# Adaptive modulation computed beside the first layer's projection instead of in a stage of its own

## The reference

```python
for layer in range(DEPTH):                      # DEPTH = 2
    mod_l = (silu(c) @ w_ada[layer] + b_ada[layer])[:, None, :]
    mod_c = (silu(c_ctx) @ w_ada[layer] + b_ada[layer])[None, None, :]
    sh_ml, sc_ml, gt_ml, sh_fl, sc_fl, gt_fl = split(mod_l, 6, axis=-1)
    ...
    a_lat = rmsnorm(h_lat, g_mix[layer]) * (1 + sc_ml) + sh_ml
    a_ctx = rmsnorm(h_ctx, g_mix[layer]) * (1 + sc_mc) + sh_mc
    # layer 0
    cq, ckv, kr, qs, ks, vs = split_last(a @ w_in, [384, 256, 32, 512, 128, 128])
    q = rmsnorm(cq, g_q) @ w_uq                 # 8 heads of 64 + 32
    kv = rmsnorm(ckv, g_kv) @ w_ukv             # 8 heads of 64 + 64
    ...
```

## Time and profile before

| | us |
|---|---|
| median of 3 runs | 3107.32 |
| lowest and highest of them | 3104.43, 3111.47 |
| the profiled execution | 3107.07 |
| its span, first to last instruction | 3105.3 |
| the modulation stage ends, the next stage's first DMA is issued | 160.5, 165.7 |
| first product of `chunk(0, 0)` | 178.2 |
| first product of the attention of layer 0 | 374.0 |

### The profile page before, as it was taken

How to read it: one execution, slowest core, us unless ns; L and a number is a source line. 1 busy time by engine, 2 the same in 40 slices (tenths; PEclk the granted TensorE clock), 3 DMA queues, 4 the chain that set the end, 5 groups by cost and what they waited for, 6 DMA issues and landing times. The chain is left out here.

```text
span 3105.3 us, 37707 instructions
## 1 busy us (share of the span) xinstructions
PE 2736.1 (88%) x12450; PEld 1942.5 (63%) x12450; DVE 1725.1 (56%) x2132; ACT 1462.1 (47%) x2059; POOL 991.4 (32%) x697
## 2 busy tenths in 40 slices
PE   7979999987879999999994679997779999999990
PEld 2345677775457676666772668885547677667660
DVE  7923244543745555656563855555465566565546
ACT  5612233431146666666662344444126666666650
POOL 1000000012345555555551000001235555555542
PEclk9989999998989999999997789998889999999995
DMA  9930100023059999999995611102329999999966
GB/s 349 354 119 14 41 1 1 1 78 151 6 208 379 386 387 370 375 373 375 382 340 190 250 55 37 37 11 85 149 76 367 374 365 342 362 348 346 358 251 257
DMA packets 160999, 694.89 MB, mean 224 GB/s; under 512 B 34776, under 2 KB 46040, under 8 KB 100752
## 3 DMA queue, kind: packets, MB, share of 16 engines
q1 hardware_dynamic: 116240, 607.41, 52.0%
q0 software_dynamic: 43520, 84.21, 7.1%
q10 hardware_dynamic: 1152, 2.11, 0.2%
HBM read 678.82 MB, written 86.08 MB: 246 GB/s over the span
## 5 line engine op out<-in xcount | busy, mean ns | idle before, releaser
L1571 DVE TENSOR_TENSOR F_gu_lo<-gu_raw,F_gu_hi 128x2048 fp32r<-128x2048 f32 x292 | 662.2, 2291 | 589.3 <-ACT F_gu_hi L1516 580.3
L1516 ACT ACTIVATE F_gu_hi<-gu_raw 128x2048 fp32r<-128x2048 f32 x292 | 554.2, 1918 | 71.8 <-DMA gu_raw<-in_we_up_dram 47.7
L1465 PE MATMUL F_psY<-d_raw,F_hT 128*128 128x512 f32 x1168 | 525.6, 593 | 2.9 <-ACT F_hT L1534 2.9
L102 PE MATMUL F_psG<-F_gu_hi,F_xT_hi 128*128 128x512 f32 x1168 | 470.5, 403 | 6.9 <-DVE F_xT_lo L1563 6.9
L104 PE MATMUL F_psG<-F_gu_hi,F_xT_lo 128*128 128x512 f32 x1168 | 458.0, 392 | 0.0
L103 PE MATMUL F_psG<-F_gu_lo,F_xT_hi 128*128 128x512 f32 x1168 | 456.5, 391 | 0.0
L1391 POOL DMA_INDIRECT F_xb<-f_d,F_gi x146 | 339.4, 2325 | 130.5 <-POOL F_gi L1388 120.5
L1465 PEld LDWEIGHTS F_psY<-d_raw,F_hT 128*128 128x128 f32 x1168 | 211.2, 191 | 212.9 <-issue 209.5
L1530 ACT ACTIVATE F_yb<-F_psY,wgt 128x1024 f32<-128x1024 f32 x146 | 163.1, 1117 | 362.2 <-PE F_psY L1465 362.2
L1388 POOL COPY F_gi<-gat 128x1 int32 (+1 forms) x146 | 303.4, 2078 | 15.4 <-PE F_psX L1448 15.1
L102 PEld LDWEIGHTS F_psG<-F_gu_hi,F_xT_hi 128*128 128x128 f32 x1168 | 221.7, 190 | 49.2 <-DVE F_xT_lo L1563 8.3
(11 more groups left out here) (335 smaller groups left out, 4430.3 us busy)
## 6 DMA issues: line engine op xcount, KB each, us to landing
gu_raw<-in_we_gate_dram SPq DMA_DIRECT2D x146, 1024.0 KB, 9.0
gu_raw<-in_we_up_dram SPq DMA_DIRECT2D x146, 1024.0 KB
d_raw<-in_we_down_dram SPq DMA_DIRECT2D x146, 1024.0 KB, 6.9
wada<-in_w_ada_dram SPq DMA_DIRECT2D x24, 2048.0 KB, 11.2
I_ring<-y_d SPq DMA_DIRECT2D x24, 1024.0 KB, 7.0
H_y<-y_d SPq DMA_DIRECT2D x4, 4096.0 KB, 18.9
I_w_raw<-in_wc_in_dram SPq DMA_DIRECT2D x32, 384.0 KB, 3.3
f_d<-D_f SPq DMA_DIRECT2D x10, 512.0 KB, 2.6
```

Of the source, the lines that this page charges most:

```text
L102: nc.tensor.matmul(acc, xh, wh, start=(start and i == 0), stop=False)
L1465: ins = nc.tensor.matmul(psY[:, n], hT[:, j, k], d_raw[:, j, k, c], start=(k == 0), stop=(k == KF - 1))
L1516: nc.scalar.activation(gu_hi[:, j, v], gu_raw[:, j, v], ACT.Copy).then_inc(s_guh, 1)
L1571: V.tensor_tensor(gu_lo[:, j, v], gu_raw[:, j, v], gu_hi[:, j, v].bitcast(F32), ALU.subtract).then_inc(s_gul, 1)
```

## The change

`stage_modulation` and the barrier behind it are gone. `stage_front(t_, wq0)` takes the place of both stages.

- The two condition vectors stand in a zero-padded stationary operand `cs`, 128 x 32 for each of the 8 slices of the contraction, in plain fp32. There is no high and low half.
- The work is cut into 48 steps: six groups of 2048 output columns (`QUADS`), each over 8 slices of the contraction (`KD`). A step reads one 128 x 2048 piece of `w_ada` (1 MB). It is four matmuls with 512 columns each, whose results go to partitions 0 to 31, 32 to 63, 64 to 95 and 96 to 127 of one PSUM bank `psM`.
- The first group, which is shift and scale of layer 0, goes first; its 8 MB have a buffer of their own, `wq0`. The other 40 steps stand one behind each product of the projection from product number 8 on (`step(g)` at the end of `chunk`). They read from a ring of two 1 MB buffers, which are tiles 2 to 5 of `h`. So `x` and `ctx` are read tile by tile into `h[:, t % 2]`, and once more, whole, at the start of `stage_attend0`, ahead of the sink values in SP's list.
- Shift and scale are no longer broadcast over partitions. The projection turns the normalized tile first; shift and scale, turned once by four PE transposes into `mc`, are applied per partition while the turned tile is brought out of PSUM, four slices by ACT and four by DVE. POOL's addition goes.
- `up(t, 0)` and `up(t, 1)` are split in two products each (`Q0`, `Q1` of 384 columns, `K0`, `K1` of 512), and share a three-buffer `psC` with the chunks. `psU` goes. One stage now has 48 products, eight for each tile.
- Bias and store of a group go through SP. The gains are loaded by POOL.

```diff
-        stage_modulation()
-        end_stage()
...
-                stage_project0(t_)
+                stage_front(t_, wq0)
...
+            QN, QUADS, RING = 2048, 6, 2
+            STEPS = QUADS * KD
...
+                cs = sb(ctx, "B_cs", [P, KD, 32])
...
-                psC = ps(ctx, "B_psC", [P, 2, 512])
+                psC = ps(ctx, "B_psC", [P, 3, 512])
...
-                psU = ps(ctx, "B_psU", [P, 1024])
...
+                ring = [h[:, 2:4].rearrange("p t d -> p (t d)"), h[:, 4:6].rearrange("p t d -> p (t d)")]
...
+                        def rows(t):
+                            if t >= 2:
+                                sp.wait_ge(s_an, t - 1)
...
+                            sp.dma_start(h[:, t % 2], src).then_inc(s_hin[t % 2], 16)
...
+                        for i in range(KD, STEPS):
+                            q, k = divmod(i, KD)
+                            if i == 10:
+                                rows(4)
+                            if i == 17:
+                                rows(5)
+                            if k == 4 and q >= 1:
+                                if q >= 2:
+                                    store(q - 1)
+                                else:
+                                    sp.wait_ge(s_mrow, q)
+                                load_bias(q)
+                            r = (i - KD) % RING
+                            if i - KD >= RING:
+                                sp.wait_ge(s_stp, i - RING + 1)
+                            sp.dma_start(ring[r], w_ada(i)).then_inc(s_rg[r], 16)
...
-                            nc.gpsimd.tensor_tensor(an[:], an[:], aadd[:], ALU.add).then_inc(s_an, 1)
...
-                                ins = nc.scalar.activation(aT[:], src, ACT.Copy)
...
+                                for k in range(KD // 2):
+                                    ins = nc.scalar.activation(aT[:, k], src[:, k], ACT.Identity, scale=mc[:, v, KD + k:KD + k + 1], bias=mc[:, v, k:k + 1])
...
-                            nc.vector.scalar_tensor_tensor(an[:], h[:, t], st[:, 0, 2:3], amul[:], ALU.mult, ALU.mult).then_inc(s_an0, 1)
+                            V.tensor_scalar(an[:], h[:, t % 2], st[:, 0, 2:3], None, ALU.mult).then_inc(s_an, 1)
...
+                        def step(i):
+
+                            q, k = divmod(i, KD)
...
+                            for j in range(4):
+                                ins = nc.tensor.matmul(psM[32 * j:32 * j + 32], cs[:, k], w[:, j * 512:(j + 1) * 512], start=(k == 0), stop=(k == KD - 1))
+                            ins.then_inc(s_stp, 1)
...
+                            if g >= KD:
+                                step(g)
...
+                        for k in range(KD):
+                            step(k)
+                            if k == 5:
+                                turn("A", 0)
+                        pe.wait_ge(s_mrow, 1)
+                        for c in range(4):
+                            ins = nc.tensor.transpose(psM[:, c * P:(c + 1) * P], mrow[:, c * P:(c + 1) * P], ident)
+                        ins.then_inc(s_mt, 1)
...
+                        sp.dma_start(h[:, 0:NL], a["x"][0].rearrange("(t p) d -> p t d", p=P)).then_inc(s_h, 16)
+                        sp.dma_start(h[:, NL:NT], a["ctx"][0].rearrange("(t p) d -> p t d", p=P)).then_inc(s_h, 16)
                         sp.dma_start(sink[:], a["wa_sink"][0:1, :].to_broadcast([P, 8])).then_inc(s_sink, 16)
```

More of the change, by code:

```diff
@@ L146, in kview @@
             return w.rearrange("(p k) n -> p k n", p=P)
[L149 to L270, removed]
-                            if i == WB:
-                                dve.wait_ge(s_cst, 16)
-                                nc.vector.tensor_copy(ident_b[:], ident)
-                                nc.vector.tensor_copy(mask_b[:, 0], cst[:, C_MP:C_MP + P])
-                                nc.vector.tensor_copy(mask_b[:, 1], cst[:, C_MN:C_MN + P])
-                        out_of(2 * NCH - 1)
@@ new lines, in w_ada, with store @@
+                        def w_ada(i):
+                            q, k = divmod(i, KD)
+                            return a["w_ada"][q // 3].rearrange("(p k) n -> p k n", p=P)[:, k, q % 3 * QN:(q % 3 + 1) * QN]
+                        def store(q):
+                            sp.wait_ge(s_mrow, q + 1)
+                            for v in range(2):
+                                sp.dma_start(mod_d[q // 3, v, q % 3 * QN:(q % 3 + 1) * QN].rearrange("(g n) -> g n", n=512),
+                                             mrow[v:P:32]).then_inc(s_mout, 16)
@@ new lines, in load_bias @@
+                        def load_bias(q):
+                            for v in range(2):
+                                sp.dma_start(bias[v:P:32], a["b_ada"][q // 3, q % 3 * QN:(q % 3 + 1) * QN].rearrange("(g n) -> g n", n=512)).then_inc(s_b, 16)
+                        sp.dma_start(craw[:, 0, :], a["c"][0].rearrange("(p k) -> p k", p=P)).then_inc(s_c, 16)
+                        sp.dma_start(craw[:, 1, :], a["c_ctx"].rearrange("(p k) -> p k", p=P)).then_inc(s_c, 16)
+                        sp.dma_start(wq0[:, 0], w_ada(0)).then_inc(s_q0[0], 16)
@@ new lines, in _, with w_chunk @@
+                        sp.dma_start(cst[:], a["cst"]).then_inc(s_cst, 16)
+                        rows(0)
+                        for k in range(1, KD):
+                            sp.dma_start(wq0[:, k], w_ada(k)).then_inc(s_q0[k], 16)
+                            if k == 1:
+                                sp.wait_ge(s_zero, 3)
+                                load_bias(0)
+                        wv = a["wa_in"][0].rearrange("(k p) n -> p k n", p=P)
+                        def w_chunk(i):
+                            c0, n = chunks[i]
@@ L372, in _ @@
+                        store(QUADS - 1)
+                        sp.wait_ge(s_mout, 32 * (QUADS - 1))
                     @block.gpsimd
                     def _(pool):
-                        for t in range(NT):
-                            pool.wait_ge(s_an0, t + 1)
-                            nc.gpsimd.tensor_tensor(an[:], an[:], aadd[:], ALU.add).then_inc(s_an, 1)
+                        nc.gpsimd.memset(cs[:], 0.0).then_inc(s_zero, 1)
+                        nc.gpsimd.memset(bias[:], 0.0).then_inc(s_zero, 1)
@@ L414, in evac @@
                             ins.then_inc(s_tev, 1)
+                        act.wait_ge(s_zero, 3)
+                        act.wait_ge(s_c, 32)
+                        for v in range(2):
+                            ins = nc.scalar.activation(cs[:, :, v], craw[:, v, :], ACT.Silu)
+                        ins.then_inc(s_silu, 1)
+                        act.wait_ge(s_cst, 16)
                         norm(0)
@@ L543, in _ @@
                                 chunk(s, 3)
-                                up_q(s)
+                                chunk(s, "Q0")
+                                chunk(s, "Q1")
                     @block.tensor
```

270 lines of the change are left out of this document (173 added, 97 removed).

## The result

The changed kernel took 3027.02 us (median of 4 runs, 3023.88 to 3031.44) against 3109.39 us for the kernel before (4 runs). The ratio is 0.9736 with a 95% interval of 0.9721 to 0.9750: 82 us faster, where 27 were forecast. Repeated on another chip, the pair gave 3025.5 and 3107.8 us, 0.9732 (0.9717 to 0.9747).

The account below looks back on a forecast made before the run. DMA was taken to bound the modulation and PE the projection. Against 3107.07 us, -142.4 + 85.8 + 13.1 - 7.1 + 14 + 1 + 8.3 = -27.3 gave 3080 us, range 3025 to 3140.

Parts of the forecast that it names:

- the full overlap of the groups: Rival for the modulation steps on PE: all four column groups stream side by side, step 0.86 us, total 3033 us; chance 0.26.
- the stepwise one: Main case for the modulation steps: PE's program order lets column groups overlap only partly, 2.15 us a step, 3080 us; chance 0.46.
- the price of a step: Forty modulation steps added to PE's list in the projection, 2.15 us each, +85.8 us; ends +34 and +137.
- Going over: PE switching between full-width products and column groups, charged 0.33 us a step: +13.1 us, bounds 0 and +21.
- The front: Everything ahead of the first projection product: `chunk(0, 0)` starts at 35.8 us instead of 178.2, -142.4 us.
- The waits for `psU`: PE's waits in the projection for DVE to empty `psU`, 5.6 + 1.5 us, go: -7.1 us.
- The stall at piece 17: In SP's list `rows(5)` waits for `norm(3)` ahead of piece 17; PE stands 11 us, with low clock +14 us (8 to 17).
- piece 10: `rows(4)` ahead of this piece in SP's list has the same form; 10.3 of 11.2 us are covered, +1 us.
- The sink values: At the attention's start their small load waits behind 3.15 MB of `x` and `ctx` on SP: +8.3 us (0 to 9.1).
- The ring getting tight: Under full overlap, close projection products leave 5 us for a piece: +1 us a tile, +5 us.
- The band of 3064 to 3094 for the likeliest case: Span of total time for partly overlapping groups, 3080 us, with all small terms at their ends; chance 0.46.
- a warm PE: Small term at the projection's start, set at zero: the first chunk may find PE's clock up, up to -3 us.

Follow-up runs that it names:

- pair experiment: Changed kernel with its first eight steps run in pairs of two contraction slices, pairs 0 and 2 slice by slice, 1 and 3 group by group: 3031.2 us in one run.

## Why the prediction was wrong, point by point

The direction was right and the measured time lies in the range, 2 us above its lower end. But the forecast of 3080 us was the wrong case: the full overlap of the groups, at 0.26, held, and not the stepwise one at 0.46. The range was drawn to take in that rival, so that it holds says nothing for the mechanism.

- **The step that failed is the price of a step**: "I take the middle", 2.15 us, +85.8. It rested on two readings of the rows: a product is two records (true: 320 records for 160 products in the forty steps), and full-width records start in program order (true, but no evidence on groups: each of those products writes all 128 partitions, so in none of them was there another group that could have gone ahead). The pair experiment shows that groups don't wait for one another. A step streams for 0.86 us, +34.3. That is 51.5 of the 55 us between the gain forecast, 27.3, and the one measured, 82.4. The prediction set two statements of the Trainium skill's page "TensorE: Matmul & The Clock Gate" against each other. The speedup of 2.38 times for three column groups, in its section "Measured speedup vs the span model", points the right way: four groups here take 0.99 against 3.43 us, 3.5 times. The statement of the same page of the Trainium skill, in "The mechanism", that matmuls start in program order did not hold here for two products per group: the first record of the next group started 14 ns behind the first of its predecessor, ahead of three records that stand before it.
- **Going over**, +13.1 from two tails of 0.163: 0.28 us a step, +11.3. The size is right. It doesn't show in the step's own row alone: 0.13 us of it lies there and the rest in what stands behind. The tail is the difference to a modelled end, so that it comes so close may be luck.
- **The front**, -142.4: -144.4. The last piece was taken up at 28.5 us, a microsecond ahead of the estimate, with DMA at 342 and 392 GB/s instead of 306 and 379. The chain from there to the first product took 5.3 us instead of 6.3. (The 379 GB/s are not in the earlier trace rows; they are the kernel before's rate from 20 to 40 us.)
- **The waits for `psU`**, -7.1: gone.
- **The stall at piece 17**, +14, and piece 10, +1: 10.4 and 1.5 us of wait and about 2 of low clock. The run with the loads moved takes 14.7 us out of the projection and has neither wait. Right, by the mechanism named.
- **The sink values**, +8.3: the attention is 8.0 us longer than before, PE's wait 8.8. Right, in size and mechanism: with the order undone the attention takes 8.1 or 10.9 us less in the two traces.
- **The ring getting tight** under full overlap, +5: no such wait; a piece landed in 4.7 us (median of 40), and the two tightest places leave about 5. That rival's 3033 was 6 us too high, 5 of it by this term.
- The sum for the projection with measured terms: 195.8 + 34.3 + 11.3 + 12.0 + 2 - 7.1 = 248.3 us, which is what it took. The 2 us of low clock are mainly the step and the turns behind the wait, 1.93 and 1.94 us instead of 1.06 and 1.08. The going over was itself taken from the length of one tile, so the sum tests only that the other tiles are like it.
- The band of 3064 to 3094 for the likeliest case does not follow from its terms. With the going over and the sink values at nothing, the stall at 8 and a warm PE it reaches down to about 3050.

What makes the later stages differ by 8 us between the two profiled executions is open. The same stages spread by 12 us over the traces of kernels that don't differ in them.

## What to carry to other kernels

A stage held by DMA can go under a stage held by PE, but its worth is decided by what it adds to PE: the same change came to +11 us with steps at full width and to -82 with four column groups. Price an operation that the trace doesn't show by its two ends, and don't let a rule seen only where there is no choice (order among full-width products) pick the value between them. When loads are threaded into one queue's list, look for each wait in it and for what stands behind: two such places cost 21 us here, and both went by moving three lines.

## What the runs showed that I had not expected

- Four column groups stream four fp32 products in the time of one, whatever order the products stand in within a pair: first records 6 to 7 ns apart slice by slice, 13 to 17 ns group by group.
- Pieces of 1 MB read as 8 KB a partition moved at 418 GB/s; the kernel before read 2 MB pieces as 2 KB segments at 345 GB/s, both with DMA's share near 1. The runs did not vary the segment alone, so this is a reading and no proof.
- With two buffers of 1 MB, a consumer that keeps each for 1.9 us (58.04 us for 30 steps) got a piece each 3.4 us, 308 GB/s; with eight, one each 2.5 us.
